# The norm's sum in front of the filter's transform on TensorE, between two layers of a hybrid diffusion trunk

## The chip, the cores and the metric

The program runs on one core of one Trainium2 chip. The metric is the device time of one execution in microseconds (us); lower is better. A core has TensorE (matrix products, with a separate record for the load of its stationary operand), VectorE, ScalarE, GpSimd and SyncE, which here only issues DMA transfers. In the rows they are called PE (and PEld for the loads), DVE, ACT, POOL and SP.

## The reference

Two groups of 128 tokens with 1024 channels (context tokens and latent tokens) go through two layers with the same code and separate weights:

```python
for l in range(DEPTH):                       # DEPTH = 2
    h = rms_norm(x, norm1) * (1 + sc1) + sh1
    qa, ka, va, hy, qr, kr, vr, gr = split(h @ w_in)
    ya = diff_attention(qa, ka, va, ...)
    yb = hyena_mixer(hy, ...)                # long convolution, by FFT
    yc = bidir_retention(qr, kr, vr, ...)    # normed, gated with gr
    merged = ga * (ya @ w_branch_a) + gb * (yb @ w_branch_b) + gc * (yc @ w_branch_c)
    x = x + g1 * (merged @ w_out)
    h2 = rms_norm(x, norm2) * (1 + sc2) + sh2
    x = x + g2 * moe(h2, ...)                # 16 experts, top 2 of one group
y = rms_norm(x, final_g)
```

Two pieces of it matter here. `rms_norm` needs, for each token, the sum of x squared over the 1024 channels:

```python
y = xf * lax.rsqrt(jnp.mean(xf * xf, axis=-1, keepdims=True) + EPS)
```

And the Hyena branch convolves with a filter of its own, which a small network makes out of positions alone, and which is multiplied in the frequency domain: `ff = jnp.fft.rfft(filt, n=2 * L, axis=0)`. The filter depends on the layer's weights and not on the tokens.

## The kernel before

All numbers are float32. Channels lie on the 128 partitions, so `x` and `h` are 8 tiles of 128 channels x 256 tokens (both groups side by side). Every engine has its own program, written out by hand in the order in which it runs; engines meet at semaphores. TensorE works strictly through its list, and its order is the order of the calls from line 1216 on.

The weights (some 350 MB) are read from DRAM in pieces of 1 MB into 8 ring slots and some lent buffers, by SyncE's queue, in the fixed order of `PLAN`. A piece is issued once TensorE has given back the slot it goes to (`s_weights_used`).

A layer is, on TensorE: the norm's sum, the first projection units, the other projection and gate units with attention, FFT and retention between them, merge, output projection, router, and then seven items of experts (`moe_in`, `moe_out`). Each item's result is added over experts in `combine` (line 1162) into banks 0 to 3.

At the boundary between the layers these steps follow on one another:

- VectorE copies the last upper half of the experts' result (`out_high`, line 2238); TensorE runs the last four matmuls of `combine` (line 1169).
- VectorE adds the result to `x`, 16 instructions at line 2377, and signals `s_x_moe` after each pair of tiles.
- ScalarE squares each pair of tiles into `h` (`squares`, line 1309, the instruction at 1316) and signals `s_x_squared`, four times.
- `norm_sum` on TensorE (line 815) multiplies the 8 tiles of squares by a matrix of ones into bank 4, and waits for `s_x_squared` at every second tile. One matmul in the program leaves two records in the trace.
- VectorE takes the mean (`norm_mean`, line 1675), ScalarE the root (line 1321), VectorE the reciprocal (line 1681) and the scaling of each tile (line 1685), and VectorE and ScalarE, each for one of the two groups, scale and shift (lines 1687 and 1330) and signal `s_h_ready_v` and `s_h_ready_s` for each tile.
- `first_units(1)` on TensorE (line 877) runs projection units 0 and 1 together, tile by tile, as the tiles of `h` come (records at line 847). It also waits for the weights of both.

The filter for the next layer is made in five steps, `filter_step(layer, 0)` to `(layer, 4)` at line 776. The first four run between the experts' items, as their small network needs VectorE and ScalarE in turn. Step 4, called the filter's transform here, has six matmuls of 128x128 by 128x512 into banks 5, 6 and 7 (lines 811 and 812). It waits for the taps (`s_taps`) and for the banks; ScalarE copies the three banks in the third unit of layer 1 (line 1443).

In the kernel before, TensorE runs the transform behind the last `combine`, and `norm_sum(1)` behind the transform, at the head of the next turn of the loop:

```python
for layer in range(DEPTH):
    norm_sum(layer)
    ...
        if layer + 1 < DEPTH:
            filter_step(layer + 1, 4)
norm_sum(DEPTH)
```

Of the kernel before, what the change touches and what calls it, by code (L numbers as in the profile page):

```python
# [23 lines left out]
DEPTH = 2  # L24
# [283 lines left out]
def trunk_program(nc, row_scratch, cond_scratch, weights, mod_weights, cond_rows, experts, mod_params, params, consts, shared, x_in, k_cache, v_cache, s_cache,  # L308
                  y_out, k_out, v_out, s_out):
    with ExitStack() as ctx:  # L310
# [416 lines left out]
        def _(pe):  # L727
# [4 lines left out]
            def take(b):  # L732

                if held[b]:
                    pe.wait_ge(s_bank_free[b], held[b])
                held[b] += 1
# [8 lines left out]
            def spin(b, n):  # L745

                take(b)
                for _ in range(n):
                    last = pe.matmul(bank[b][:, 0:P], ones[:, :], ones[:, :], start=True, stop=True)
                last.then_inc(s_bank_free[b], 1)  # L750

            def ada(layer, q, b):

                w = [piece(256) for _ in range(4)]
                take(b)
                for k in range(KT):
                    for j in range(4):
                        last = pe.matmul(bank[b][32 * j:32 * j + 32, 0:256], condT[:, k, :],  # L760
                                         w[j][:, k, :], start=(k == 0), stop=(k == KT - 1),
                                         skip_group_check=True)
                last.then_inc(s_weights_used, 4)

            def ada_turn(layer, q, b):
                n = ada_at(layer, q)
                if n == 0:
                    pe.wait_ge(s_ident_in, 16)
                pe.wait_ge(s_mod_rows_copied, n + 1)
                take(b)  # L770
                for t in range(2):
                    last = pe.transpose(bank[b][:, t * P:(t + 1) * P],
                                        mod_row[:, n % 2, t * P:(t + 1) * P], ident)
                last.then_inc(s_mod_sum, 1)
# [40 lines left out]
            def norm_sum(count):  # L815
                take(4)
                for k in range(KT):
                    if k % 2 == 0:
                        pe.wait_ge(s_x_squared, 4 * count + k // 2 + 1)
                    last = pe.matmul(bank[4][:, 0:TOK], ones[:, :], h[:, k, :], start=(k == 0),  # L820
                                     stop=(k == KT - 1))
                last.then_inc(s_norm_sum, 1)

            def proj(layer, u):
                b = u % 4
                w = piece(256)
                take(b)
                if U_VR <= u < U_QA or U_VA <= u < U_GR:
                    for g in range(GROUPS):
                        for k in range(KT):  # L830
                            last = pe.matmul(bank[b][:, g * 256:(g + 1) * 256], h[:, k, g_cols(g)],  # L831
                                             w[:, k, :], start=(k == 0), stop=(k == KT - 1))
                else:
                    for c in range(2):
                        for k in range(KT):
                            last = pe.matmul(bank[b][:, c * TOK:(c + 1) * TOK],  # L836
                                             w[:, k, c * P:(c + 1) * P], h[:, k, :],
                                             start=(k == 0), stop=(k == KT - 1))
                last.then_inc(s_weights_used, 1)
# [12 lines left out]
            def first_units_of_first():  # L852

                w = []
                for u in range(3):
                    w.append(piece(256))
                    take(u)
                    for k in range(4):
                        proj_part(0, u, w[u], k)
                    filter_step(0, u)  # L860
                ada(0, 1, 6)
                w.append(piece(256))
                take(3)
                for k in range(2):
                    proj_part(0, 3, w[3], k)
                ada_turn(0, 1, 7)
                for k in range(2, 4):
                    proj_part(0, 3, w[3], k)
                filter_step(0, 3)
                for u in range(4):  # L870
                    for k in range(4, KT):
                        last = proj_part(0, u, w[u], k)
                    last.then_inc(s_weights_used, 1)
                    if u == 1:
                        filter_step(0, 4)

            def first_units(layer):

                w = [piece(256), piece(256)]
                take(0)  # L880
                take(1)
                for k in range(KT):
                    for u in range(2):
                        last = proj_part(layer, u, w[u], k)
                        if k == KT - 1:
                            last.then_inc(s_weights_used, 1)
# [327 lines left out]
                last.then_inc(s_more_combined[layer], 1)  # L1214

            pe.wait_ge(s_ones_set, 2)
            for layer in range(DEPTH):
                norm_sum(layer)
                if layer == 0:
                    pe.wait_ge(s_cond_ready, 1)  # L1220
                    spin(6, 16)
                    ada(0, 0, 4)
                    ada_turn(0, 0, 5)
                    first_units_of_first()
                else:
                    first_units(layer)
                for u in range(U_MERGE):
                    if u >= (2 if layer else 4):
                        proj(layer, u)
                    if u == 7:  # L1230
                        z_transpose(layer, 0)
                    if u == 9:
                        dft(layer, 0)
                    if u == 10:
                        z_transpose(layer, 1)
                    if u == 11:
                        ret_scores(layer, 0)
                    if u == 12:
                        dft(layer, 1)
                    if u == 13:  # L1240
                        idft(layer, 0)
                    if u == 14:
                        ret_out(layer, 0)
                    if u == 15:
                        idft(layer, 1)
                        o_norm(layer, 0)
                    if u == 16:
                        ret_scores(layer, 1)
                    if u == 17:
                        k_transpose(layer)  # L1250
                        ret_out(layer, 1)
                    if u == 18:
                        o_norm(layer, 1)
                        states(layer)
                    if u == 25:
                        o_norm(layer, 2)
                    if u in SCORES_AT:
                        att_scores(layer, SCORES_AT.index(u))
                    if u - 1 in SCORES_AT:
                        att_turn(layer, SCORES_AT.index(u - 1))  # L1260
                    if u - 2 in SCORES_AT:
                        att_out(layer, SCORES_AT.index(u - 2))
                merge(layer)
                out_proj(layer)
                route(layer)
                tokens_turn(layer)
                spin(2, 8)
                ranks(layer)
                spin(2, 5)
                gather(layer, 0)  # L1270
                for p in range(ITEMS):
                    moe_in(layer, p)
                    if p < PAIRS:
                        gather(layer, p + 1)
                    act_turn(layer, p)
                    if p:
                        moe_out(layer, p - 1)
                    if layer + 1 < DEPTH and p >= 3:
                        filter_step(layer + 1, p - 3)
                pe.wait_ge(s_more_known, layer + 1)  # L1280
                blocks = pe.value_load(ints[0:1, 0:1], min_val=0, max_val=MORE)
                moe_out(layer, PAIRS)
                leave.append((nc.cur_bb, blocks, list(held)))
                pe.br_lt(blocks, 1, on_true=f"pe_on{layer}", on_false=f"pe_more{layer}_0")
                on = nc.switch_bb(f"pe_on{layer}")
                if layer + 1 < DEPTH:
                    filter_step(layer + 1, 4)
            norm_sum(DEPTH)
            pe.br("pe_end")
            for layer, (here, blocks, taken) in enumerate(leave):  # L1290

# [1216 lines left out]
```

## Time and profile before

| | us |
|---|---|
| median of 3 runs | 1157.66 |
| lowest and highest | 1155.68 to 1158.28 |
| span of the profiled execution | 1155.5 |
| TensorE matmul busy | 1100.4 (95%) |
| VectorE busy | 542.0 (47%) |
| ScalarE busy | 209.8 (18%) |
| read from DRAM | 346.08 MB, 302 GB/s over the span |

The span runs from the first to the last instruction of one profiled execution, and times in the rows count from its start. The page lists the engines' busy time, the span in slices, the DMA queues, and a chain of work that ended last, which is followed back from the last instruction; a wait is charged to what released it. Matmul records of one line overlap: the duration of one record is longer than the distance between two, so work is best counted by the distance between starts, which is what the chain shows.

### The profile page before, as it was taken

What the parts mean: (1) busy time and instruction counts of PE and PEld (TensorE: products, weight loads), DVE (VectorE), ACT (ScalarE), POOL (GpSimd) and SP (SyncE); (2) the same over time, 40 slices, a digit from 0 to 9 for tenths busy, and PEclk for the clock granted to TensorE, in tenths of its full rate; (3) what the DMA queues carried; (4) which work ended last, traced back from release to release, by engine and by line L of the source; (5) the groups of instructions that cost most, each with busy time, mean ns of one, the idle gap of its engine ahead of it and who ended that gap; (6) DMA issues with size and microseconds to landing.
All of it is one profiled execution on the core that took longest, in us unless ns stands there. A gap on an engine that the chain in (4) does not pass through costs nothing.

```text
span 1155.5 us, 15668 instructions
## 1 busy us (share of the span) xinstructions
PE 1100.4 (95%) x6026; PEld 783.7 (68%) x6026; DVE 542.0 (47%) x1202; ACT 209.8 (18%) x440; POOL 41.0 (4%) x83
## 2 busy tenths in 40 slices
PE   6999999999999999999889999999999999999965
PEld 4688888878887445454358888888888844545422
DVE  2469887677846311121244886646543551111003
ACT  3251022232021101111025111323201210000001
POOL 1001110000000000000000111000000000000000
PEclk9999999999998999999999999999999899999999
DMA  9657865467587999999955677437347979999993
GB/s 382 284 204 279 326 221 227 168 270 272 219 350 318 419 420 422 420 421 421 421 219 201 215 276 285 174 133 283 139 145 306 375 305 421 421 420 421 421 420 121
DMA packets 56943, 351.38 MB, mean 304 GB/s; under 512 B 7088, under 2 KB 7264, under 8 KB 20512
## 3 DMA queue, kind: packets, MB, share of 16 engines
q1 hardware_dynamic: 52704, 337.75, 73.5%
q0 software_dynamic: 4160, 12.58, 3.0%
q8 instruction: 50, 0.82, 0.3%
q14 instruction: 29, 0.24, 0.1%
HBM read 346.08 MB, written 2.65 MB: 302 GB/s over the span
## 4 chain that ended last, share of the span: by engine, by line
PE 84%; DMA 8%; DVE 3%; SPq 3%; ACT 1%; issue 1%; DVEq 0%; ACTq 0%
PE bank L836 26%; PE bank L1127 15%; PE bank L1016 7%; PE bank L1148 6%; DMA ring<-in_experts 5%; PE bank L1037 5%; PE bank L831 5%; PE bank L1112 5%; PE bank L1169 3%; PE bank L847 3%; DMA ring<-in_weights 3%; SPq L615 2%; PE bank L760 1%; PE bank L820 1%; PE bank L961 1%
## 5 line engine op out<-in xcount | busy, mean ns | idle before, releaser
L836 PE MATMUL bank<-h,ring 128*128 128x256 f32 x1472 | 324.8, 380 | 0.0
L836 PEld LDWEIGHTS bank<-h,ring 128*128 128x128 f32 x1472 | 277.4, 190 | 40.1 <-issue 3.2
L1750 DVE SCALAR_TENSOR_TENSOR ring<-ring 128x1024 f32<-128x1024 f32 x160 | 189.5, 1222 | 18.7 <-DMA ring<-in_mod_weights 9.1
L1127 PE MATMUL bank<-ring,gates 128*32 128x512 f32 (+2 forms) x616 | 137.7, 614 | 8.8 <-DMA h<-in_experts 5.0
L1127 PEld LDWEIGHTS bank<-ring,gates 128*32 128x32 f32 (+2 forms) x616 | 41.2, 126 | 69.5 <-issue 69.1
L1127 PE MATMUL bank<-lent,gates 128*32 128x512 f32 (+2 forms) x408 | 81.4, 593 | 2.0 <-ACTq L1618 2.0
L2238 DVE COPY uc_zt_dsum<-bank 128x512 f32<-128x512 f32 x14 | 9.7, 692 | 122.8 <-PE bank L1148 122.8
L1148 PE MATMUL bank<-ring,gates 128*32 128x512 f32 (+1 forms) x240 | 64.4, 595 | 2.0 <-issue 1.2
L1148 PE MATMUL bank<-lent,gates 128*32 128x512 f32 (+2 forms) x304 | 60.5, 594 | 1.3 <-DMA ring<-in_experts 1.0
L1112 PE MATMUL bank<-uc_zt_dsum,gates 128*128 128x128 f32 x448 | 55.5, 285 | 1.0 <-DVEq L2246 1.0
L1127 PEld LDWEIGHTS bank<-lent,gates 128*32 128x32 f32 (+2 forms) x408 | 25.2, 123 | 46.2 <-issue 43.7
L1016 PE MATMUL bank<-lent,ring 128*128 128x256 f32 x256 | 56.4, 380 | 0.0
L831 PE MATMUL bank<-ring,h 128*128 128x256 f32 x256 | 56.2, 379 | 0.0
L1169 PEld LDWEIGHTS bank<-gates,uc_zt_dsum 128*128 128x128 f32 x224 | 41.4, 190 | 21.1 <-issue 16.1
L1037 PE MATMUL bank<-uc_zt_dsum,ring 128*128 128x256 f32 x256 | 55.6, 379 | 0.0
L1169 PE MATMUL bank<-gates,uc_zt_dsum 128*128 128x256 f32 x224 | 52.3, 385 | 3.4 <-DVE uc_zt_dsum L2238 1.8
L1112 PEld LDWEIGHTS bank<-uc_zt_dsum,gates 128*128 128x128 f32 x448 | 54.2, 201 | 1.4 <-issue 1.4
L1670 DVE SCALAR_TENSOR_TENSOR gates<-gates,bank 128x512 f32<-128x512 f32 x14 | 9.6, 687 | 93.3 <-issue 75.8
L1037 PEld LDWEIGHTS bank<-uc_zt_dsum,ring 128*128 128x128 f32 x256 | 48.6, 190 | 6.6
L1016 PEld LDWEIGHTS bank<-lent,ring 128*128 128x128 f32 x256 | 48.5, 190 | 6.5
L831 PEld LDWEIGHTS bank<-ring,h 128*128 128x128 f32 x256 | 48.2, 190 | 6.3
L1662 DVE TENSOR_TENSOR gates<-gates,bank 128x512 f32<-128x512 f32 x14 | 9.6, 687 | 85.5 <-PE bank L1127 85.5
(271 smaller groups left out, 1203.7 us busy)
## 6 DMA issues: line engine op xcount, KB each, us to landing
ring<-in_experts SPq DMA_DIRECT2D x93, 1024.0 KB, 19.8
ring<-in_weights SPq DMA_DIRECT2D x85, 1024.0 KB, 7.7
lent<-in_experts SPq DMA_DIRECT2D x72, 1024.0 KB, 17.8
ring<-in_mod_weights SPq DMA_DIRECT2D x80, 512.0 KB, 5.1
h<-in_experts SPq DMA_DIRECT2D x10, 1024.0 KB, 19.4
uc_zt_dsum<-in_experts SPq DMA_DIRECT2D x10, 1024.0 KB, 19.5
va_vr<-in_experts SPq DMA_DIRECT2D x7, 1024.0 KB, 12.2
lent<-in_weights SPq DMA_DIRECT2D x3, 1024.0 KB, 23.5
```

The lines of the kernel that those rows point to most:

```text
L615: sp.dma_start(slot_of(n), source).then_inc(s_weights_in[SLOT[n]], 16)
L760: last = pe.matmul(bank[b][32 * j:32 * j + 32, 0:256], condT[:, k, :], w[j][:, k, :], start=(k == 0), stop=(k == KT - 1), skip_group_check ...
L831: last = pe.matmul(bank[b][:, g * 256:(g + 1) * 256], h[:, k, g_cols(g)], w[:, k, :], start=(k == 0), stop=(k == KT - 1))
L836: last = pe.matmul(bank[b][:, c * TOK:(c + 1) * TOK], w[:, k, c * P:(c + 1) * P], h[:, k, :], start=(k == 0), stop=(k == KT - 1))
L847: last = pe.matmul(bank[u][:, c * TOK:(c + 1) * TOK], w[:, k, c * P:(c + 1) * P], h[:, k, :], start=(k == 0 and c == 0), stop=(k == KT - 1 ...
L1016: last = pe.matmul(bank[b][:, c * TOK:(c + 1) * TOK], w[:, k, d * P:(d + 1) * P], src[:, k, :], start=(k == 0), stop=(k == 3))
L1037: last = pe.matmul(out[c], w[:, k, c * P:(c + 1) * P], merged[:, k, :], start=(k == 0), stop=(k == KT - 1))
L1112: last = pe.matmul(bank[4 + half][:, c * P:(c + 1) * P], htok[:, g, k * P:(k + 1) * P], pick[p % 2][:, g, :], start=(g == 0), stop=(g == 1))
L1127: last = pe.matmul(bank[b][rows, :], hgat[:, 4 * half + f, rows], w[j][:, f, :], start=(half == 1 and f == 0), stop=(half == 0 and f == 3) ...
L1148: last = pe.matmul(bank[5 - half][rows, :], actT[p % 2][:, f, rows], w[j][:, f, :], start=(f == 0), stop=(f == 3), skip_group_check=True)
L1169: last = pe.matmul(bank[dt // 2][:, (dt % 2) * TOK:(dt % 2 + 1) * TOK], ysb[:, dt * P:(dt + 1) * P], matrix, start=(fresh and dt % 2 == 0) ...
L1750: last = dve.scalar_tensor_tensor(out, w, 0.5, cond_wide[:, c, :], ALU.mult, ALU.mult, accum_out=mod_all[:, of, row, c:c + 1])
```

## The change

The call of `norm_sum` moves from the head of the loop to its foot, in front of `filter_step(layer + 1, 4)`. The first call stands ahead of the loop now, and the last one is inside.

```diff
             pe.wait_ge(s_ones_set, 2)
+            norm_sum(0)
             for layer in range(DEPTH):
-                norm_sum(layer)
                 if layer == 0:
                     pe.wait_ge(s_cond_ready, 1)
                     spin(6, 16)
...
                 pe.br_lt(blocks, 1, on_true=f"pe_on{layer}", on_false=f"pe_more{layer}_0")
                 on = nc.switch_bb(f"pe_on{layer}")
+                norm_sum(layer + 1)
                 if layer + 1 < DEPTH:
                     filter_step(layer + 1, 4)
-            norm_sum(DEPTH)
             pe.br("pe_end")
```

TensorE's program between the layers, before. L1169 is the last `combine`, L1284 the branch that is taken when no expert had more tokens than its room, L811 and L812 are the filter's transform, L820 is the norm's sum, L847 the first projection units; what stands in brackets are the semaphores that an instruction waits for.

```order
L1169 MATMUL bank<-gates,uc_zt_dsum 128x256 x3
L1284 COMPARE_AND_BRANCH
L811 MATMUL bank<-va_vr,cst 128x512 [waits bank_free5,taps_decayed_scaled]
L812 MATMUL bank<-va_vr,cst 128x512
L811 MATMUL bank<-va_vr,cst 128x512 [waits bank_free6]
L812 MATMUL bank<-va_vr,cst 128x512
L811 MATMUL bank<-va_vr,cst 128x512 [waits bank_free7]
L812 MATMUL bank<-va_vr,cst 128x512
L820 MATMUL bank<-h,ones 128x256 [waits x_squared,bank_free4]
L820 MATMUL bank<-h,ones 128x256
```

The same place in the changed program:

```order
L1284 COMPARE_AND_BRANCH
L820 MATMUL bank<-h,ones 128x256 [waits x_squared,bank_free4]
L820 MATMUL bank<-h,ones 128x256
L820 MATMUL bank<-h,ones 128x256 [waits x_squared]
L820 MATMUL bank<-h,ones 128x256
L820 MATMUL bank<-h,ones 128x256 [waits x_squared]
L820 MATMUL bank<-h,ones 128x256
L820 MATMUL bank<-h,ones 128x256 [waits x_squared]
L820 MATMUL bank<-h,ones 128x256
L811 MATMUL bank<-va_vr,cst 128x512 [waits bank_free5,taps_decayed_scaled]
L812 MATMUL bank<-va_vr,cst 128x512
```

The eight matmuls of the sum moved ahead of the six of the transform, and their waits with them; the transform now stands directly in front of L847. On TensorE nothing else has another place: the sum at the opening and the one at the end follow and precede the same instructions as before. The lists of VectorE, ScalarE, GpSimd and SyncE are unchanged.

## Rows read from the trace of the kernel before

**Rows 1.** The page: the chain that ended last, by engine.

```profile
PE 84%; DMA 8%; DVE 3%; SPq 3%; ACT 1%; issue 1%; DVEq 0%; ACTq 0%
```

**Rows 2.** Chain of waits between the layers: start us, us, what.

```profile
582.91 1.97 PE bank L1169 x8
584.88 0.86 PE bank L811 x2
...
589.17 0.86 PE bank L812 x2
590.03 3.47 PE bank L820 x16
...
593.52 0.43 DVE rmsi L1667
...
597.53 15.68 PE bank L847 x64
613.21 6.91 PE bank L836 x32
```

**Rows 3.** Timeline of VectorE and ScalarE there: start us, us, engine, line, instruction.

```profile
583.01 4.22 DVE L1670 SCALAR_TENSOR_TENSOR x<-bank,modT,x 128x128 f32<-128x128 f32 x16 [0.25 <-DVE uc_zt_dsum L2238]
584.17 0.63 ACT L1316 ACTIVATE h<-x 128x512 f32<-128x512 f32 x1 [8.77 <-DVE x L1670]
...
587.27 0.63 ACT L1316 ACTIVATE h<-x 128x512 f32<-128x512 f32 x1 [0.40 <-DVE x L1670]
587.92 1.28 ACT L1321 ACT_TABLE_LOAD   x1
...
598.25 0.49 ACT L1330 ACTIVATE h<-h,modT,amp 128x128 f32<-128x128 f32 x1 [0.22 <-DVE h L1662]
598.97 0.49 ACT L1330 ACTIVATE h<-h,modT,amp 128x128 f32<-128x128 f32 x1 [0.22 <-DVE h L1662]
...
621.07 1.57 ACT L1443 ACTIVATE lent<-bank 128x512 f32<-128x512 f32 x3
```

**Rows 4.** Timeline at the end of the kernel, from the last combine on.

```profile
1139.69 1.96 PE L1169 MATMUL bank<-gates,uc_zt_dsum 128*128 128x256 f32 x8 [0.90 <-DVE uc_zt_dsum L2238]
...
1143.68 0.73 PEld L820 LDWEIGHTS bank<-h,ones 128*128 128x128 f32 x4 [0.30 <-ACT h L1316]
1144.04 0.63 ACT L1316 ACTIVATE h<-x 128x512 f32<-128x512 f32 x1 [0.40 <-DVE x L1670]
...
1145.89 0.42 DVE L1667 TENSOR_SCALAR rmsi<-bank 128x256 f32<-128x256 f32 x1 [1.88 <-PE bank L820]
1146.50 0.42 ACT L1321 ACTIVATE tmp<-rmsi 128x256 f32<-128x256 f32 x1 [0.53 <-DVEq L1677]
```

**Rows 5.** Waits of TensorE, 579 to 600 us: in total, times, longest.

```profile
PE bank L847 <- ACT h L1330: 4.0, 1, 4.0
PE bank L1169 <- DVE uc_zt_dsum L2238: 0.9, 1, 0.9
```

**Rows 6.** Stretches: us, busy of PE, PEld, DVE, ACT, POOL, PEclk, DMA share, GB/s.

```profile
584.90:590.00 5.10, 5.10 (x13) 2.23 (x13) 2.34 (x10) 3.17 (x4) 0.00 (x0) 1.00 0.99 419
593.50:597.50 4.00, 0.00 (x0) 0.00 (x1) 3.27 (x5) 0.91 (x2) 0.00 (x0) 0.99 0.71 283
597.50:600.80 3.30, 3.27 (x8) 2.67 (x9) 3.12 (x11) 2.38 (x5) 0.00 (x0) 0.50 0.00 0
600.80:613.20 12.40, 12.40 (x59) 10.93 (x58) 1.31 (x4) 1.90 (x5) 0.00 (x0) 1.00 0.01 1
...
1139.70:1145.90 6.20, 6.09 (x24) 4.11 (x24) 4.24 (x17) 3.74 (x5) 0.00 (x0) 1.00 0.01 3
```

**Rows 7.** DMA issue of projection unit 1's weights, and its time to landing.

```profile
L615 SPq DMA_DIRECT2D ring<-in_weights x1: 338/338/338, 574.8 to 574.8; - x1
...
DMA to landing us min/median/max: 8.3/8.3/8.3
```

**Rows 8.** Layer 1's router and experts: stretches, and SyncE's issue behind the pause.

```profile
918.30:925.10 6.80, 6.80 (x32) 6.61 (x32) 3.77 (x10) 0.00 (x0) 0.00 (x0) 0.50 0.45 186
...
922.00:930.90 8.90, 8.90 (x51) 6.45 (x52) 6.32 (x22) 0.60 (x1) 0.00 (x0) 0.83 0.01 3
930.90:1134.90 204.00, 191.97 (x1202) 91.00 (x1198) 34.31 (x107) 18.71 (x34) 0.00 (x0) 0.99 0.99 412
...
930.92 0.80 SPq L615 DMA_DIRECT2D ring<-in_experts  x2
...
PE bank L1076 <- DVE rt L1662: 2.1, 1, 2.1
```

## Prediction, made before the changed kernel ran

> **What bounds the kernel now.** I read the page's shares first, then the chain of work that ended last, first whole and then cut to the boundary between the two layers. TensorE carries 84% of that chain [rows 1], so what matters is whether an edit shortens the chain where TensorE is waited for. At the boundary the chain runs [rows 2]: the filter's transform, six pieces of 0.86 us from 584.88 (the six stand one behind the other, the last at 589.17), then the norm's sum of 3.47 us from 590.03, then VectorE and ScalarE with mean, root, reciprocal, scale and shift, then the first two projection units of layer 1 from 597.53. The reader is to see that the transform stands in front of a sum for which a long chain on the other engines waits, while nobody waits for the transform soon: ScalarE takes its results at 621.07 [rows 3], 31 us behind its end. TensorE itself then has nothing to do for 4.0 us; it waits for ScalarE's first finished tile [rows 5]. That idle stretch is the cover into which the transform can be moved.
>
> **What the change does, step by step.** Nothing is added or removed: 8 matmuls of the sum (16 records, since each float32 matmul leaves two) change places with 6 of the transform (12 records). Waits move with them. DMA issues, VectorE, ScalarE and the other queues keep their order.
>
> Step 1, the sum comes earlier. It needs the squares, in four pieces, and bank 4. The residual adds run on VectorE from 583.01 for 4.22 us, the first square ends at 584.17 + 0.63 = 584.80, the last at 587.27 + 0.63 = 587.90 [rows 3]. The combine before it on TensorE ends at 584.88 [rows 2]. So the sum can start at once and then goes at the pace of the squares. The end of the kernel shows just this arrangement, with nothing between combine and sum [rows 4]: there the combine starts at 1139.69, the last square at 1144.04, and the mean at 1145.89, that is 6.20 us behind the combine's start and 1.85 behind the last square's. Taken to the boundary (combine at 582.91, last square at 587.27) this gives 589.11 and 589.12; now it is 593.52. The mean starts **4.4 us earlier**. The wait for the squares that the change puts in front of the transform is in that number; behind it on TensorE stand the transform and the first units.
>
> Step 2, the chain behind the mean. From the mean at 593.52 to the first projection matmul at 597.53 it is 4.01 us [rows 2]. ScalarE's table for the root is loaded from 587.92 for 1.28 us, to 589.20 [rows 3], while the mean would end at 589.12 + 0.43 = 589.55: the load stays hidden, by 0.35 us, as it does at the end of the kernel where the root starts 0.6 us behind the mean's start [rows 4]. The first tile is ready for TensorE at 589.12 + 4.01 = 593.13.
>
> Step 3, the transform in its new place. The sum ends on TensorE at about 589.09 and the transform takes 590.03 - 584.88 = 5.15 us. It ends at 594.24, 1.11 us behind the first tile. So of its 5.15 us, 4.04 lie in the cover and 1.11 on the path, and the first units start at 594.24 instead of 597.53: **3.3 us earlier**. By then tile 2 of 8 is ready (they come every 0.7 us [rows 3], and the units use one in 13.82 / 8 = 1.7 us), so tiles hold nothing up. What would be late next is not the norm but the transform itself.
>
> Step 4, the clock. In the idle stretch the granted clock is still 0.99; in the next 3.3 us it is 0.50, the 1.2 GHz level, and then 1.00, the 2.4 GHz level [rows 6]. So the first units, 64 records, take 15.68 us, where the 32 records of the next unit take 6.91 [rows 2], which makes 13.82 for 64. The fall costs 1.86 us. After the change TensorE has a pause of 0.9 us in front of the combine, which is there now too [rows 5], and three between the squares, of up to 0.3 us at the end of the kernel [rows 4]. That broken sum ran at 1.00 throughout [rows 6]. I take the fall as gone: **1.9 us** more.
>
> Sum at the end of the first units: 594.24 + 13.82 = 608.06 against 613.21, **5.15 us earlier**. That this equals the whole of the transform is chance; it is 3.29 of waiting and 1.86 of clock.
>
> Bounds: if the fall were not there in other runs of the kernel before, or stayed after the change, step 4 is nothing and the gain 3.3. If the chain behind the mean took less than 4.01, nothing changes, since the transform ends later. If the sum fell at half clock for its last pair of tiles (0.87 us at full clock), the transform would start 0.9 later.
>
> A rule that speaks against the change is in the Trainium skill, "TensorE: Matmul & The Clock Gate", section "A second HAM failure mode: psum-queue depth-cycling": short idle moments between groups of matmuls can make the clock swing between its two levels, even without one long pause. The row of the broken sum at 1.00 [rows 6] does not bear it out for its four groups. By the rule the clock would fall again here, and the sum would be 3.3 instead of 5.15; it is the second case below, whose time is worked out from rows alone.
>
> **Is it carried to the end?** The weights of the first two units are no hindrance: the second is issued at 574.80 and lands 8.3 us later, at 583.1 [rows 7], before either start. From 600.8 to 613.2 the DMA queues are all but empty [rows 6], and later loads wait for slots that TensorE gives back. In layer 1 the experts' stream is the bound: 204 us at 412 GB/s. But just before it the DMA engines stand at 0.01 for 8.9 us, with all slots full, and the stream starts with an issue at 930.92, right behind the first experts' use by TensorE [rows 8]. So the start of the stream moves with TensorE, and its length stays. I carry 5.15 us to the end: 1155.5 - 5.15 = 1150.4 for the span of the profiled execution. This span is 2.2 us below the median of 1157.66; the page does not tell whether that is time outside the span or the spread between runs (1155.68 to 1158.28), so I take the difference off the median: 1157.66 - 5.15 = **1152.5 us**.
>
> **Rivals.** (1) The wait goes, the clock does not. The sum's gaps let the clock fall once, for as long as now, or the timed runs of before lack the fall. Then the gain is 3.3: 1154.3 us. For it: TensorE has less dense work between 581 and 589 than now. Against: the 1.00 in the broken sum at the end [rows 6].
>
> (2) The gain is swallowed in layer 1. At the router stage the clock was at 0.50 for 6.8 us [rows 8], behind a wait of TensorE for VectorE; such a stretch costs 3.4 us in front of the experts' stream. Work that comes 5 us earlier may meet it in another place and lose more there, or some load may set the stream's start after all. Then 1157.7. Against: the idle DMA engines in front of 930.92.
>
> (3) Slower: the low clock over the whole moved piece. Place: from the last pair of squares on. If the clock falls in the broken sum and stays low over the transform, the last pair costs 0.87 more, the transform 5.15 more, and the first units begin low for 3.3 us as they do now (1.86). Against the full gain of 5.15 that is 7.9 lost: 1157.66 + 2.7 = 1160.4 us. It decides from the point at which the clock is low for more than 10.3 us in all, since half of low time is lost. The longest low stretch that I found is 6.8 us [rows 8], and while the transform ran in its old place, from 584.9 on, the clock was at 1.00 [rows 6].
>
> (4) The change does not do what it says. The order of TensorE's instructions shows that it does; the other two sums (opening and end) keep their place. 1157.7.
>
> **How the numbers follow.** My forecast has 0.72, rival 1 0.14, rival 2 0.09, rival 3 0.04, rival 4 0.01. The forecast's own range is 1150.8 to 1154.0: the runs of before lie up to 2.0 us below and 0.6 above their median, and a low stretch more or less elsewhere is worth 1.7. To hold 8 in 10 the range must take in rival 1 with some spread, so it is 1150.6 to 1155.2. A measurement of this kernel can tell about 0.2%, 2.3 us, from no change, so faster means below 1155.3: the forecast and nearly all of rival 1, 0.85. Within 0.2%: the rest of rival 1, rivals 2 and 4, 0.11. Slower: rival 3, 0.04.
>
> **What would show it.** In the changed kernel's profile the mean follows the last square's start by 1.85 us (step 1); the transform lies between the sum and the first units without a gap, and TensorE's wait of 4.0 us for the first tile is gone (steps 2 and 3); the first units take 13.8 us and the granted clock beside them is 1.00 (step 4); the experts' stream starts about 5 us earlier, by an issue near 925.8, and still takes 204 us. I am wrong if the root waits for its table, if the transform waits for something new, if the clock is low anywhere between 585 and 608, or if the stream's issue does not move.

## The result, and the profile after

| | us |
|---|---|
| changed kernel, first comparison: median of 4 runs | 1149.76 (1148.73 to 1152.94) |
| before, beside it: median of 4 runs | 1156.95 (1155.68 to 1158.28) |
| ratio, 95% interval | 0.9944 (0.9928 to 0.9960) |
| span of the changed kernel's profiled execution | 1151.0, with a time of 1152.94 |

The change makes the kernel faster, by 6.5 us by the ratio (4.6 to 8.3). Three of the four runs of before are those of the first table. The forecast was 1152.5 us with a range from 1150.6: the direction was right, the median lies 0.8 us below the range.

The chain of waits of the changed kernel at the boundary (start us, us, what), which answers to [rows 2]:

```profile
585.01 1.97 PE bank L1169 x8
...
587.04 4.14 PE bank L820 x16
591.19 0.86 PE bank L811 x2
...
596.34 13.81 PE bank L847 x64
610.15 14.89 PE bank L836 x69
```

L1169 is the last combine, L820 the norm's sum, L811 (with L812) the transform, L847 the first units. The norm's sum stands directly behind the last combine and takes 4.14 us, at the pace of the squares. The transform follows without a gap, and the units follow the transform. VectorE and ScalarE are off the chain. From the combine's start to the end of the units it is 610.15 - 585.01 = 25.14 us, where [rows 2] give 613.21 - 582.91 = 30.30: **5.16 us less**. The timeline of the other engines answers to [rows 3] and [rows 4]:

```profile
589.37 0.63 ACT L1316 ACTIVATE h<-x 128x512 f32<-128x512 f32 x1 [0.40 <-DVE x L1670]
590.02 1.28 ACT L1321 ACT_TABLE_LOAD   x1
...
591.22 0.42 DVE L1667 TENSOR_SCALAR rmsi<-bank 128x256 f32<-128x256 f32 x1 [1.88 <-PE bank L820]
...
591.84 0.42 ACT L1321 ACTIVATE tmp<-rmsi 128x256 f32<-128x256 f32 x1 [0.54 <-DVEq L1677]
...
594.60 0.49 ACT L1330 ACTIVATE h<-h,modT,amp 128x128 f32<-128x128 f32 x1 [2.34 <-DVE h L1662]
```

The mean (L1667) starts 1.85 us behind the last square's start (L1316), as at the end of the kernel. The root (L1321) does not wait for its table, and the first tile (L1330) is finished at 595.09, 1.25 us ahead of the units. The stretches (us; busy of PE, PEld, DVE, ACT and POOL; granted clock, DMA share and GB/s) answer to [rows 6] and [rows 8]:

```profile
587.00:591.00 4.00, 3.96 (x16) 2.91 (x17) 2.34 (x10) 2.87 (x4) 0.00 (x0) 1.00 1.02 420
591.20:596.30 5.10, 5.10 (x13) 2.24 (x13) 4.29 (x9) 1.84 (x5) 0.00 (x0) 1.00 1.00 418
596.30:610.10 13.80, 13.80 (x66) 12.18 (x65) 3.41 (x11) 3.40 (x8) 0.00 (x0) 1.00 0.15 61
906.80:910.10 3.30, 3.30 (x17) 3.30 (x18) 1.69 (x10) 0.95 (x3) 0.00 (x0) 0.50 1.03 427
...
926.30:1130.30 204.00, 191.89 (x1202) 91.16 (x1198) 34.09 (x106) 18.70 (x34) 0.00 (x0) 0.99 1.00 412
```

SyncE's issue, which answers to 930.92 in [rows 8]:

```profile
926.32 0.80 SPq L615 DMA_DIRECT2D ring<-in_experts  x2
```

The granted clock is 1.00 over sum, transform and units. The experts' stream is issued 4.6 us earlier in this execution (926.32 against 930.92), although the last combine started 2.1 us later in it, and the 204 us behind it again show 412 GB/s. At the router the clock is low for 3.3 us in this execution, not for 6.8 as in [rows 8].

**Where the rest of the difference lies.** The chain gives four points that every profile has: the start of the last combine of layer 0, the end of the first units, the first matmul of layer 1's experts (L1127), and the end. "Boundary" is the stretch from the first of them to the second. All seven profiles of the two kernels, those of the experiments below included, cut there (us):

| profile | to the combine | boundary | layer 1 to its experts | experts to the end |
|---|---|---|---|---|
| before | 582.91 | 30.30 | 314.08 | 228.2 |
| before, second | 581.47 | 30.35 | 313.13 | 228.3 |
| before, third | 580.90 | 30.29 | 314.10 | 228.3 |
| before, fourth | 581.04 | 30.32 | 314.11 | 228.2 |
| changed | 585.01 | 25.14 | 312.55 | 228.3 |
| changed, second | 580.14 | 25.14 | 313.09 | 228.2 |
| changed, third | 579.63 | 25.14 | 312.35 | 228.4 |

The boundary differs between the kernels by 5.2 us and within a kernel by 0.06 at most. The first column holds work that both kernels do alike, and it alone spreads over 5.4 us. The third spreads over 1.8.

### The profile page after: what moved, and what is told of

It reads as the page before. It is cut to its first block, busy times and chain, and to the rows that moved or that the text cites. A ratio compares the mean times of both kernels' runs of the same rounds, so it can differ in the third digit from the quotient of the medians.

```text
span 1151.0 us, 15668 instructions
## 1 busy us (share of the span) xinstructions
PE 1100.1 (96%) x6026; PEld 783.8 (68%) x6026; DVE 542.4 (47%) x1202; ACT 209.7 (18%) x440; POOL 41.0 (4%) x83
## 4 chain that ended last, share of the span: by engine, by line
PE 86%; DMA 7%; DVE 3%; SPq 1%; ACT 1%; issue 1%; DVEq 0%; ACTq 0%
PE bank L836 27%; PE bank L1127 15%; PE bank L1016 7%; PE bank L1148 7%; DMA ring<-in_experts 5%; PE bank L1037 5%; PE bank L831 5%; PE bank L1112 5%; PE bank L1169 3%; PE bank L847 3%; DMA ring<-in_weights 2%; SPq L615 1%; PE bank L820 1%; PE bank L760 1%; PE bank L961 1%
## 5 line engine op out<-in xcount | busy, mean ns | idle before, releaser
L1127 PE MATMUL bank<-ring,gates 128*32 128x512 f32 (+2 forms) x616 | 137.7, 614 | 8.8 <-DMA h<-in_experts 5.0
L1127 PEld LDWEIGHTS bank<-ring,gates 128*32 128x32 f32 (+2 forms) x616 | 41.3, 127 | 69.4 <-issue 69.1
L1127 PE MATMUL bank<-lent,gates 128*32 128x512 f32 (+2 forms) x408 | 81.4, 594 | 2.0 <-ACTq L1618 2.0
L1148 PE MATMUL bank<-ring,gates 128*32 128x512 f32 (+1 forms) x240 | 64.4, 595 | 1.9 <-issue 1.2
L1148 PE MATMUL bank<-lent,gates 128*32 128x512 f32 (+2 forms) x304 | 60.5, 594 | 1.3 <-DMA ring<-in_experts 1.0
L1127 PEld LDWEIGHTS bank<-lent,gates 128*32 128x32 f32 (+2 forms) x408 | 25.3, 123 | 46.1 <-issue 43.6
L1169 PEld LDWEIGHTS bank<-gates,uc_zt_dsum 128*128 128x128 f32 x224 | 41.5, 190 | 20.9 <-issue 16.1
L1169 PE MATMUL bank<-gates,uc_zt_dsum 128*128 128x256 f32 x224 | 52.3, 386 | 3.4 <-DVE uc_zt_dsum L2238 1.8
```

Source lines behind the costliest of these rows:

```text
L1127: last = pe.matmul(bank[b][rows, :], hgat[:, 4 * half + f, rows], w[j][:, f, :], start=(half == 1 and f == 0), stop=(half == 0 and f == 3) ...
L1148: last = pe.matmul(bank[5 - half][rows, :], actT[p % 2][:, f, rows], w[j][:, f, :], start=(f == 0), stop=(f == 3), skip_group_check=True)
L1169: last = pe.matmul(bank[dt // 2][:, (dt % 2) * TOK:(dt % 2 + 1) * TOK], ysb[:, dt * P:(dt + 1) * P], matrix, start=(fresh and dt % 2 == 0) ...
```

## The experiments

My theory, T1, was that the whole gain arises between the layers: 3.3 us of TensorE's wait and 1.9 us of low clock. T2 was that layer 1 gains too, T3 that the low clock in the first profile was an accident, and T4, formed later, that it often lasts longer. Each experiment is one more program or one more set of runs; "the units" are the first projection units of layer 1. The ratios below are to runs of the kernel before on the same chip.

**Both kernels once more.** No edit.

> The kernel before, once more. My theory (T1: the whole gain arises between the layers, 3.3 us of TensorE's wait and 1.9 us of low clock; what lies beyond 5.15 us is low clock elsewhere that differs from run to run): ratio 1.000 to itself within 0.2%; from the last combine's start to the end of the first units 30.3 us if the clock falls again in the 4.0 us pause, 28.4 if it does not. Router stage, from its first matmul to the first experts' matmul: anything from 18 to 22 us, another number than 21.4. Rival T2 (the change also shortens the router stage for good, by 1.5 us): the router stage is 21.4 us again. Rival T3 (the fall of the clock between the layers was an accident of one profile): 28.4 us between the layers.

> The changed kernel, once more. T1: 5.2 us (4.6 to 6) below before, ratio 0.9955; 25.1 us from the last combine's start to the end of the first units; router stage again anything from 18 to 22 us. T2: ratio 0.9940 and the router stage at 19.9 us. T3: ratio 0.9970.

Measured: before against itself 0.9999 (0.9986 to 1.0012), median 1155.89 us of 12 runs. The changed kernel 0.9957 (0.9942 to 0.9971), median 1151.50 of 10 runs against 1156.56 of 33: 5.0 us. The chain of the changed kernel's second profile:

```profile
580.14 1.97 PE bank L1169 x8
...
582.17 4.14 PE bank L820 x16
...
591.46 13.81 PE bank L847 x64
605.28 19.86 PE bank L836 x92
```

Again 25.14 us. And the kernel before, second profile, in stretches around the pause:

```profile
592.10:596.00 3.90, 0.00 (x0) 0.00 (x0) 3.19 (x5) 0.91 (x2) 0.00 (x0) 1.00 0.69 275
596.10:600.60 4.50, 4.50 (x13) 3.69 (x14) 4.28 (x13) 3.16 (x7) 0.00 (x0) 0.62 0.00 0
```

TensorE is idle, and then the clock is low for part of the next 4.5 us. T3 is out. T2 wanted a ratio of 0.9940 and 1.5 us in layer 1. The ratio's interval just leaves out 0.9940, and the two profiles of this pair show 313.13 and 313.09 us there. But the other profiles of the table differ in that column, so T2 is not out as a whole; what lies behind the column is told further down.

**The pause filled, order as before.**

```diff
                 norm_sum(layer)
+                if layer:
+                    spin(2, 17)
                 if layer == 0:
```

> The order of before, and in TensorE's pause behind the norm's sum 17 matmuls of ones by ones into bank 2, whose result nobody reads (about 3.7 us at full clock): the wait stays, the pause goes. T1: the first units start 14.6 us behind the combine as in before, and take 13.8 us instead of 15.7; 1.9 us below before, ratio 0.9984. T3 (clock no part of it): ratio 1.000. If the fillers reach beyond the first tile, they cost what sticks out, under 0.5 us.

Measured: 0.9974 (0.9962 to 0.9985), 3.0 us below before (1.7 to 4.4). Stretches of the fillers and of the units:

```profile
591.70:595.70 4.00, 3.78 (x34) 3.59 (x33) 3.27 (x5) 0.91 (x2) 0.00 (x0) 1.00 0.68 274
595.70:609.80 14.10, 14.07 (x65) 12.45 (x66) 4.44 (x14) 4.29 (x9) 0.00 (x0) 1.00 0.00 1
```

The units start at 595.73, 14.61 us behind the combine's start at 581.12, just as in before, and they take 14.05 us where they took 15.68. They are not quite at 13.8 only by the way the chain counts. Here it counts from the first record's start, behind a wait; in the changed kernel it counts from 596.34, and the first record starts at 596.17:

```profile
596.17 6.42 PE L847 MATMUL bank<-h,ring 128*128 128x256 f32 x29
```

From there it is 13.98 us to the end of the units in the changed kernel, against 14.05. Nothing but useless work was added, and the kernel is faster: the clock's part is shown, as 1.6 us in the profile. The timed gain is larger than this, though its interval reaches down to 1.7.

**The transform behind the units.**

```diff
                     first_units(layer)
+                    filter_step(layer, 4)
...
                 norm_sum(layer + 1)
-                if layer + 1 < DEPTH:
-                    filter_step(layer + 1, 4)
```

> The norm's sum in front as in the changed kernel, but the filter's transform behind the first projection units instead of in front of them, so that it no longer lies in the pause. T1: the mean still comes 4.4 us earlier than in before, but the pause of 4.0 us and the low clock are back, and the transform of 5.15 us stands on the path behind the units: transform ended 31.0 us behind the combine's start, 0.7 us later than in before, ratio 1.0007 (1.0005 to 1.001), against 0.9955 for the changed kernel. A rival in which the early sum alone is what pays expects the ratio of the changed kernel, 0.995.

Measured: 1.0016 (1.0005 to 1.0027), 1.8 us above before (0.6 to 3.1). The chain and two stretches of this kernel:

```profile
580.51 1.97 PE bank L1169 x8
...
586.72 0.44 DVE rmsi L1666
...
590.74 15.45 PE bank L847 x64
606.18 0.86 PE bank L811 x2
```

```profile
586.70:590.70 4.00, 0.00 (x0) 0.00 (x0) 3.27 (x5) 1.01 (x3) 0.00 (x0) 0.93 1.02 427
590.70:593.60 2.90, 2.86 (x7) 2.36 (x8) 2.73 (x9) 1.97 (x4) 0.00 (x0) 0.51 1.00 407
```

This is the first tile's true time: the units start 10.23 us behind the combine's start, 1.1 us ahead of the changed kernel's 11.33. And still they end later, at 25.67 against 25.14, because without the transform in front the pause of 4.0 us is back and the clock falls behind it. So the early sum alone is worth nothing here. What pays in the changed order is that the 5.15 us of the transform lie in the pause. The transform ends 30.82 us behind the combine's start, 0.5 later than all of it in before.

**A longer transform.**

```diff
                         take(b)
+                        if layer:
+                            pe.matmul(bank[b][:, :], C(a0), hs[:, 0, :], start=True, stop=True)
                         pe.matmul(bank[b][:, :], C(a0), hs[:, 0, :], start=True, stop=False)
```

> The changed kernel with a transform half as long again: three further matmuls of 128x128 by 128x512, each computed and then overwritten by the same product. 2.6 us more work for TensorE at the boundary. My theory (T1: the cover behind the norm's sum is 4.0 us, and the transform sticks out of it by 1.1 us already): all 2.6 us are on the path, 27.7 us from the last combine's start to the end of the first units instead of 25.14; 2.6 us above the changed kernel, ratio to before 0.998. Rival (there is cover left, or TensorE does not set the start of the units): 25.1 us and the changed kernel's ratio of 0.9957.

Measured: 0.9965 (0.9953 to 0.9977), 4.0 us below before. The expected ratio, 0.998, lies just outside the interval. The chain:

```profile
581.24 1.97 PE bank L1171 x8
...
608.95 13.17 PE bank L838 x61
```

From 581.24 to 608.95 it is 27.71 us, 2.57 more than in the changed kernel: every us of added transform is on the path, and the cover is used up. The profile decides this. By it the kernel should be 2.6 us below before (30.30 - 27.71), which is at the very edge of the timed interval; the timed gain is 1.4 us larger, and the profile does not say why.

**Two pieces of the transform in earlier pauses.** `early_half(b)` is the first matmul of bank b's pair, which `filter_step(1, 4)` then leaves out. After an overflow of the experts' rooms it is done again.

```diff
                     if p == PAIRS:
+                        if half and layer + 1 < DEPTH:
+                            take(7)
+                            early_half(7)
                         combine(s_y_lo, ...)
+                        if not half and layer + 1 < DEPTH:
+                            pe.wait_ge(s_taps, 2 * (layer + 1) + 2)
+                            take(6)
+                            early_half(6)
```

> The changed kernel, with two of the transform's six matmuls (0.86 us each) moved further ahead, into two pauses of TensorE of 0.9 and 0.8 us behind and in front of the last two combines of layer 0. T1: the transform behind the sum is 3.43 us instead of 5.15 and no longer sticks out of the cover of 4.04 us; the units start as the first tile comes, 1.1 us earlier than in the changed kernel; 24.0 us from the last combine's start to the end of the first units instead of 25.14, if the two pieces fit their pauses; what does not fit comes later by as much ahead of the combine (up to 0.2 us each). Ratio to before 0.9947. Rival: the pieces delay the last combine by their whole 1.7 us, and the result is 0.6 us above the changed kernel.

Measured: 0.9942 (0.9924 to 0.9960), 6.7 us below before. The interval holds the forecast and the changed kernel. The chain:

```profile
574.87 1.97 PE bank L1181 x8
576.83 0.86 PE bank L817 x2
577.69 3.57 PE bank L1153 x32
581.26 1.06 PE bank L817 x2
582.32 1.81 PE bank L1181 x8
...
592.39 14.05 PE bank L852 x64
606.44 15.76 PE bank L841 x73
```

Of the two pauses one was not there. TensorE stood still between the second to last combine and the last products (L1148) only where those products' weights came late, by 0.6 to 0.9 us in five of the seven profiles of the two kernels. The first profile of before, and then the second of the changed kernel, where the products follow the combine at once (as in the second of before):

```profile
578.38 3.64 PE L1148 MATMUL bank<-ring,gates 128*32 128x512 f32 x32 [0.86 <-DMA ring<-in_experts]
```

```profile
573.70 1.97 PE bank L1169 x8
575.66 3.62 PE bank L1148 x32
```

So the piece put there cost its own length. From the start of the second to last combine it is 31.57 us to the end of the units (574.87 to 606.44), and 31.58 in the second profile of the changed kernel (573.70 to 605.28): no gain, and no loss. In an execution in which the weights come late the piece might cost less; no profile of this kernel shows one.

**One piece.** The same with the piece of bank 7 alone, in front of the last combine, where the wait for the taps now stands too.

> The changed kernel, with one of the transform's six matmuls moved into the 0.9 us pause in front of the last combine, which every profile so far shows. The transform behind the sum is then 4.3 us and sticks out of the cover by 0.25 us. From the start of VectorE's last copy to the end of the first units: 25.1 us (changed kernel 25.98), from the start of the second to last combine 35.1 in place of 35.95. 0.9 us below the changed kernel, ratio to before 0.995 (0.9935 to 0.9965, as far as the clock's luck allows). Rival (the piece delays the combine by its own length): 26.0 and 35.95 us, the changed kernel's ratio.

Measured: 0.9951 (0.9933 to 0.9969), 5.7 us below before. (The 35.95 us that the expectation counts from "the second to last combine" are really counted from the products in front of it, 569.32 in the second profile of the changed kernel; the same count gives 35.10 here, as forecast.) The chain:

```profile
576.29 1.97 PE bank L1178 x8
...
581.82 1.05 PE bank L817 x2
582.88 1.82 PE bank L1178 x8
...
593.20 13.81 PE bank L852 x64
607.01 15.11 PE bank L841 x70
```

From 576.29 to 607.01 it is 30.72 us, 0.86 less than the 31.58 of the changed kernel: the piece fits this pause and its whole length is won. Counted so, it is the shortest of the profiles in which the products follow at once. The timed ratio cannot show so little beside the runs' spread: it is no better than the changed kernel's own.

**Fillers in two other places.**

```diff
+                spin(7, 7)
                 ada(0, 1, 6)
...
-                spin(2, 8)
+                spin(2, 12)
```

> The changed kernel with matmuls of ones, whose result nobody reads, in two other places where TensorE waits and the profiles show low clock behind: 7 in front of the second modulation product of the opening, and 4 more (12 instead of 8) in the router stage of both layers. T1 says nothing but this: if low clock in these places makes the spread from run to run, fillers narrow it and bring 0 to 3 us below the changed kernel, ratio 0.993 to 0.9957. Rival (the spread has another cause, or the stretch of low clock begins ahead of the pause that is filled): ratio as the changed kernel's 0.9957 or above, as fillers that overrun their pause delay what follows, by up to 1 us each.

Measured: 0.9949 (0.9933 to 0.9966), 6 runs between 1149.51 and 1153.25 us. That is the changed kernel's value, with no narrower spread: inconclusive, and no way to a better kernel. Its profile shows one effect: the clock is at 1.00 in the opening, where each of the other profiles has at least one low stretch of 3.4 us.

```profile
12.00:45.00 33.00, 28.66 (x240) 21.66 (x239) 10.33 (x29) 5.06 (x10) 1.19 (x3) 1.00 0.89 368
```

But the last combine of layer 0 starts at 582.22, no earlier than in profiles with the low stretch (579.63 to 585.01), and layer 1's router stage, which has more fillers too, still has low clock. The boundary is 25.13 us.

**The changed kernel a third time**, beside the one piece.

> The changed kernel a third time, beside the kernel above. My theory (5.15 us, all between the layers): ratio 0.9955, within 0.9940 to 0.9970; 25.14 us from the last combine's start to the end of the first units. The rival that the first comparison, 0.9944, shows a further gain in layer 1: 0.9944 or below.

Measured: 0.9934 (0.9911 to 0.9957), 6 runs. The point is on the rival's side and the interval holds both. The boundary is 25.14 us once more.

**Two more looks at before.**

> The kernel before, one more profile, for what the low clock between the layers lasts. Over all timed runs so far the changed kernel lies 6.1 us below before (5.2 to 7.1), 1 us more than the 5.15 us of the two profiles. Theory T4 (the low stretch behind the pause is longer in some executions than the 3.4 us of the profiles): 30.3 us from the last combine's start to the end of the first units, or 32 with a stretch of 6.8 us. Rival T1 (it is 3.4 us always; the rest is luck elsewhere): 30.3 us.

> As the one ahead, a second look at the kernel before: T4 30.3 or 32 us, T1 30.3 us. If either of the two shows 32, T4 is shown; if neither does, it stays open.

Measured: 30.29 and 30.32 us; the two times are 1155.55 and 1155.64 us. From the first of them, the chain and two stretches:

```profile
595.52 15.67 PE bank L847 x64
611.19 16.84 PE bank L836 x78
```

```profile
594.00:597.30 3.30, 1.78 (x4) 1.51 (x5) 3.12 (x10) 1.81 (x4) 0.00 (x0) 0.71 0.11 42
597.30:600.70 3.40, 3.40 (x14) 2.83 (x13) 2.74 (x9) 2.13 (x5) 0.00 (x0) 0.78 0.00 0
```

There is one low stretch behind the pause in each of the four profiles of before, and the units take 15.67 to 15.74 us. T4 is not shown.

**The late transform, pause filled.**

```diff
                 norm_sum(layer + 1)
+                if layer + 1 < DEPTH:
+                    spin(2, 17)
```

> The transform behind the first units, as in the experiment that came out 0.16% slower than before, and now 17 matmuls of ones, which nobody reads, in the pause behind the norm's sum. The waits stay as there, the pause goes. T1 (the fall costs 1.7 to 1.9 us): 29.1 us from the last combine's start to the end of the transform instead of 30.82, and 1.7 us less time than that experiment, ratio 1.0001. T4 (the fall costs 2.6 to 3 us on the average of runs): the same in the profile, but a ratio of 0.9990. Both are far from the changed kernel's 0.995, since the 5.15 us of the transform are on the path here.

Measured: 0.9999 (0.9986 to 1.0012), 0.17% or 2.0 us below the same kernel with its pause (the two were measured on different chips, each against before; both intervals together leave some 0 to 4 us). In the profile the transform ends 29.42 us behind the combine's start (580.44 to 609.86), 1.4 less than 30.82. A second order of instructions, and the same worth of a filled pause. By their ratios T1 and T4 are 1.3 us apart here, and the interval holds both.

## Why the prediction was right in its steps and wrong in its number

The mechanism is as forecast, and the miss lies in the number that the gain was taken off, and in the range.

**Step 1, the sum earlier: right.** The mean was forecast 6.20 us behind the last combine's start, and came 591.22 - 585.01 = 6.21 behind it.

**Step 2, the chain behind the mean: right.** The experiment with the late transform shows the first tile's use 590.74 - 586.72 = 4.02 us behind the mean; forecast 4.01. The table stayed hidden.

**Step 3, the transform in the pause: right.** The units were forecast 594.24 - 582.91 = 11.33 us behind the combine's start, and came 11.33 behind it. That 1.1 us stick out is shown from both sides: 2.57 us more of transform cost 2.57, and 0.86 us less gave 0.86.

**Step 4, the clock: right in what it does, a little high in its price.** The units take 13.81 us where 13.82 was forecast. Filling the pause alone brings 1.6 us in the profile of one order and 1.4 in that of the other, not 1.86. The 1.86 compares units behind a wait (15.68) with units behind other products (13.82), and these are counted from different points, as the filled pause shows (14.05 with the clock at 1.00). So 1.63 of it is the clock and 0.23 goes with the start behind a wait, which the changed order removes as well. The sum is right as forecast, 5.16 us in the profiles; only its split is off.

**Carried to the end: right** as a mechanism. Experts to the end is 228.2 to 228.4 us in all seven profiles. The prediction left open whether the 2.2 us between span and time are outside the span. They mostly are: in every run on record the time is 1.75 to 2.10 us above the span.

**The number: wrong**, by 2.75 us, and three terms of it add up to that. The first is the base. I took 5.15 us off the median of 3 runs, 1157.66, and noted their spread without using it for the base; over all 91 runs of before it is 1156.31, so 1.35 us of the miss were there before the change came in. (A fourth run beside the first three already brought that median to 1156.95.) The second is the sample of the changed kernel: 4 runs gave 1149.76, all 20 give 1150.29, another 0.53. The third, 0.87, is what all runs together show beyond the forecast: medians 6.0 us apart, by means 6.0 as well (5.0 to 7.0, all chips together).

**The step that failed is the base of the sum, 1157.66, together with the range drawn around the result.** In 1157.66 - 5.15 the second term measured 5.16 in the profiles, and the first measured 1156.31. The range did not make up for it. I named two sources of spread, runs "up to 2.0 us below and 0.6 above their median" and one low stretch "more or less elsewhere", worth 1.7. Below 1152.5 the first alone reaches 1150.5, and both together reach 1148.8; the range that I wrote down ends at 1150.6, and its own terms do not give that. The measured 1149.76 lies between. The runs of before really go from 1153.77 to 1160.43. Two rows show one source. They cover the opening, at the second modulation product, in the changed kernel's first profile and then in its second, 39.8 to 46.5 us in each:

```profile
39.80:46.50 6.70, 5.75 (x56) 3.14 (x60) 0.00 (x0) 0.00 (x0) 0.00 (x0) 0.50 0.15 61
```

```profile
39.80:46.50 6.70, 5.75 (x75) 4.29 (x76) 0.56 (x1) 1.44 (x2) 0.53 (x1) 1.00 0.27 83
```

The modulation product starts at 40.75 and 40.76 us, and runs at half and at full clock; the projection units that follow start at 47.19 us in the one and at 44.35 in the other, 2.8 apart. The first profile of before lies between, with 0.75 in this stretch, and the other four have 1.00. The router stages add more of it. Low clock is not all of the spread, though: the second profile of before has a lower mean clock than the first (0.981 against 0.984) and a span that is 2.2 us shorter (1153.3 against 1155.5), so the amount of low clock alone does not order the runs. With these runs in hand I would estimate a range of about 1149 to 1155.

**The rivals.** Rival 1 (the clock does not recover) is out: 1.00 beside sum, transform and units. Rival 3 is out with it: none of the changed kernel's three profiles has a low stretch there. The rule of the Trainium skill ("TensorE: Matmul & The Clock Gate", section "A second HAM failure mode: psum-queue depth-cycling") is not borne out here for the four groups of the sum. That is a mild test. The pauses of "up to 0.3 us" that the prediction names are those of the weight loads (the PEld row of [rows 4]), and the matmuls beside them are busy for 3.96 of 4.00 us. Rival 4 is out by the chain. Rival 2 (swallowed in layer 1) is out too, and it pointed the wrong way.

**What stays open** is whether the 0.87 us is real. The forecast's 5.15 is within the interval of both repeats of the changed kernel, but by means it is near the lower end. A part of it may lie in the third column of the table, and there the record shows the place: the clock of the router stage. The rows are the third profile of before, the second of the changed kernel and its third:

```profile
916.30:923.10 6.80, 6.80 (x32) 6.61 (x32) 3.77 (x10) 0.00 (x0) 0.00 (x0) 0.50 0.43 180
```

```profile
901.60:908.40 6.80, 6.80 (x33) 6.80 (x33) 4.20 (x23) 1.27 (x3) 0.00 (x0) 0.50 0.96 399
```

```profile
901.60:905.00 3.40, 3.40 (x18) 3.40 (x18) 2.11 (x12) 0.78 (x3) 0.00 (x0) 0.50 1.01 422
```

The column follows them. It is 314.1 us in the three profiles of before with 6.8 us of low clock that starts 305 us behind the units' end; 313.1 in the second of either kernel, with 6.8 us that start some 296 behind it; and 312.4 and 312.6 in the first and third of the changed kernel, with 3.4 us at that place and 1.00 behind it. The longer transform has 3.4 us of it too, and 312.4. So in these eight profiles the column goes with the clock. The place counts as well, or something not found does: with one piece moved it is 314.0 us, with 6.8 us of low clock that start 295 behind the units' end. Whether the changed order has less low clock there for a reason or by luck is open: before has 6.8 us in four of four profiles, the changed kernel in one of three, and both kernels with the transform behind the units, which have the early sum as well, have 6.8 again. More profiles would be needed.

## What to carry to other kernels

Work that nobody waits for soon belongs behind the work that other engines wait for, so that it fills the time until they answer; its worth is the part of the pause that it fills plus what the clock loses behind that pause. Count both from rows, and count what sticks out. Moving the urgent work forward alone can be worth nothing, as the late transform shows. And when a forecast is a small difference taken off a median of three runs, that median is a term of the sum with an error of its own: here it was larger than the error of the difference.

## What the runs showed of the hardware

A pause of TensorE of 4.0 us cost more than itself: in four of four profiles of before, and in the one with the late transform, the granted clock was at 0.50 for about 3 us of the work behind it, and 34 records of useless products in the pause made the kernel 3.0 us faster (1.7 to 4.4), of which the profile shows 1.6.

Low clock does not need an idle TensorE. In the second profile of before, TensorE is busy for 3.19 of the 3.40 us ahead of the fall, in part with products of 16 columns. It is busy for all of the low stretch of the router stage behind it, with products of 16 and 128 columns:

```profile
904.30:907.70 3.40, 3.19 (x29) 3.07 (x27) 1.62 (x5) 1.20 (x4) 0.00 (x0) 1.00 1.02 422
907.80:914.60 6.80, 6.80 (x33) 6.80 (x33) 3.67 (x21) 1.62 (x3) 0.00 (x0) 0.50 1.02 420
```

Such stretches come at other places, or not at all, in the next execution, and they are one source of the several us by which runs of this kernel differ. A pause of TensorE behind a transfer, like the one in front of the last products, is in five of the seven profiles and not in the other two: one profile is not enough to build on it.
